# Two transformer stacks on one core: three tiles per operand slice, projections ahead of the gate, scaling on VectorE, and no barrier behind the setup

## What is computed

```python
h = rms_norm(x, norm_pre[l]);  u = h @ w_in[l]       # three attentions and their gates
y = g0 * ((oa*silu(a_z)) @ w_br_a) + g1 * ((ob*silu(b_z)) @ w_br_b) + g2 * ((oc*silu(c_z)) @ w_br_c)
x = x + rms_norm(y @ w_out[l], norm_post[l])
x = x + sigmoid(x @ w_ple_gate[l]) * (p[l] @ w_ple_proj[l])     # the "per-layer" stage
```

```python
x = x + rmsnorm(m, norm_mix_post[layer])                        # m: retention or dilated attention
f = conv_ffn(rmsnorm(x, norm_ffn_pre[layer]), ...)              # (gelu(conv(h @ w_gate)) * (h @ w_val)) @ w_down
x = x + rmsnorm(f, norm_ffn_post[layer])
if layer == 0: k_sh, v_sh = shared_kv(x, kv_norm, att_w_kv, pos)
```

## Time and profile before

| | |
|---|---|
| median of three runs | 3306.7 us (3305.99 to 3308.75) |
| the profiled execution | 3308.05 us, of it 3306.2 us in the span |
| busy: TensorE, VectorE, Pool, ScalarE | 92%, 58%, 36%, 32% of the span |
| mean granted TensorE clock | 0.972 of full |
| read from memory | 257.6 MB, 80 GB/s over the span |

### The profile page before, as it was taken

How to read it: one execution, slowest core, us unless ns; L and a number is a source line. 1 busy time by engine, 2 the same in 40 slices (tenths; PEclk the granted TensorE clock), 3 DMA queues, 4 the chain that set the end, 5 groups by cost and what they waited for, 6 DMA issues and landing times.

```text
span 3306.2 us, 38334 instructions
## 1 busy us (share of the span) xinstructions
PE 3058.2 (92%) x15088; PEld 2362.2 (71%) x15088; DVE 1909.6 (58%) x2974; ACT 1054.6 (32%) x1826; POOL 1200.1 (36%) x520
## 2 busy tenths in 40 slices
PE   5989999979899999789999989998799999979997
PEld 3766777767667777677776868886577777768885
DVE  4676554555765554555444488823666666488832
ACT  3433333234333432332222232223333333332221
POOL 2322333443222334432232444444333333244443
PEclk9999999989999999999999989999899999999998
DMA  5222222313222223232222323331222222223331
GB/s 164 64 77 64 64 77 83 90 51 99 68 74 67 71 76 90 70 98 68 64 64 64 94 70 98 96 96 51 93 77 77 77 71 77 65 69 97 96 96 64
DMA packets 78506, 262.20 MB, mean 79 GB/s; under 512 B 10910, under 2 KB 13598, under 8 KB 78200
## 3 DMA queue, kind: packets, MB, share of 16 engines
q1 hardware_dynamic: 78136, 257.60, 25.9%
q10 hardware_dynamic: 192, 2.16, 0.2%
HBM read 257.56 MB, written 6.09 MB: 80 GB/s over the span
## 4 chain that ended last, share of the span: by engine, by line
PE 80%; DVE 13%; issue 2%; ACT 2%; DMA 1%; SPq 1%; POOL 0%; ACTq 0%; DVEq 0%; POOLq 0%
PE bank L649 24%; PE bank L651 23%; PE bank L650 23%; PE bank L784 2%; PE bank L737 2%; DVE x_res L1596 1%; PE bank L764 1%; PE bank L915 1%; DVE rstd L1475 1%; PE bank L743 1%; DVE sq L1485 1%; PE bank L963 1%; PE bank L1001 0%; ACT w_hi L1094 0%; PE bank L902 0%
## 5 line engine op out<-in xcount | busy, mean ns | idle before, releaser
L509 POOL TENSOR_TENSOR w_lo<-w_raw,w_hi 128x1024 fp32r<-128x1024 f32 x462 | 1120.2, 2425 | 2046.3 <-ACT w_hi L1094 2045.9
L649 PE MATMUL bank<-h_hi,w_hi 128*128 128x512 f32 x2800 | 1152.9, 412 | 133.3 <-DVE h_lo L1586 53.4
L650 PE MATMUL bank<-h_lo,w_hi 128*128 128x512 f32 x2800 | 1107.3, 395 | 0.0
L651 PE MATMUL bank<-h_hi,w_lo 128*128 128x512 f32 x2800 | 1106.4, 395 | 0.0
L1094 ACT CAST w_hi<-w_raw 128x1024 fp32r<-128x1024 f32 x462 | 483.2, 1047 | 1328.2 <-PE bank L651 1287.7
L649 PEld LDWEIGHTS bank<-h_hi,w_hi 128*128 128x128 f32 x2800 | 534.4, 191 | 306.1 <-issue 156.7
L651 PEld LDWEIGHTS bank<-h_hi,w_lo 128*128 128x128 f32 x2800 | 534.3, 191 | 118.9
L650 PEld LDWEIGHTS bank<-h_lo,w_hi 128*128 128x128 f32 x2800 | 535.6, 191 | 106.1 <-issue 4.5
L1833 DVE TENSOR_SCALAR m<-bank,gains 128x512 f32<-128x512 f32 x48 | 36.0, 751 | 337.6 <-ACT ta L1276 200.3
L1214 ACT ACTIVATE probs<-probs,small_columns 128x128 f32<-128x128 f32 (+2 forms) x192 | 101.8, 530 | 249.8 <-DVE small_columns L1631 245.6
L649 PE MATMUL bank<-f_hi,w_hi 128*128 128x512 f32 x352 | 139.2, 396 | 0.0
(11 more groups left out here) (278 smaller groups left out, 3840.9 us busy)
## 6 DMA issues: line engine op xcount, KB each, us to landing
w_raw<-in_w SPq DMA_DIRECT2D x462, 512.0 KB, 3.6
bias_copies<-bias_vectors SPq DMA_DIRECT2D x12, 320.0 KB, 9.6
x_res<-in_x_t ACTq DMA_DIRECT2D x1, 2048.0 KB, 8.6
bias<-bias_copies SPq DMA_DIRECT2D x8, 256.0 KB, 5.7
bias<-bias_copies SPq DMA_DIRECT2D x16, 128.0 KB, 2.5
out_x<-x_res SPq DMA_DIRECT2D x8, 256.0 KB, 2.0
ple_raw<-in_p_t SPq DMA_DIRECT2D x2, 512.0 KB, 3.6
ret_decay<-in_decay SPq DMA_DIRECT2D x1, 1024.0 KB, 7.6
```

The costliest lines, as they stand in the source:

```text
L509: pool.tensor_tensor(WL[slot][:], RAW[slot][:], WH[slot][:].bitcast(F32), ALU.subtract).then_inc(sems["lo_done"], 1)
L649: pe.matmul(banks[bank][:], WH[slot][:, w], hi[:, k, :], start=start, stop=False)
L650: pe.matmul(banks[bank][:], WH[slot][:, w], lo[:, k, :], start=False, stop=False)
L651: pe.matmul(banks[bank][:], WL[slot][:, w], hi[:, k, :], start=False, stop=stop).then_inc(sems["kt_done"], 1)
```

## The change

1. `linear` behind the mixes makes three tiles together instead of two, as do the feed-forwards; in the dilated stage three of the first operand and then two of the second.
2. The per-layer stage makes the eight projections of `p` first. ScalarE moves them to a new buffer `PP`, and TensorE's banks are then freed by ScalarE's semaphores (`open_for`) and no longer by VectorE's. The operand of `p` is split in `linear`, ahead of its first tile.
3. VectorE scales the tiles of `m` itself; Pool's `scale` is gone.
4. `linear` on ScalarE ends with a square root of one column, which is not used.
5. In the feed-forward the squares are multiplied out behind the fifth tile. In the dilated stage TensorE sums the eight tiles of squares itself, ScalarE makes the second operand's upper halves between the first's, and the variance is taken after four of the second's lower halves.
6. The stage "setup" is gone: its parts stand in mix0. The table of the bias has a semaphore of its own and is loaded with the gains ahead of the weights, `X` comes in two loads, the angles and lambda are made behind the lower halves and squares of the first operand, and SyncE issues the spreading of the bias vectors as two copies, the sinks behind them, and three weight chunks behind these.

The diff, cut to its core ("..." marks what is left out; all of the removed barrier, the order of the weight stream and the renamed semaphores follow from it):

```diff
-STAGES = ["setup"]
+STAGES = []
...
-            for dst, src in ((G[:], d["gains"]), (COLS[:], d["columns"]), (ID[:], d["ident"]),
...
-                sp.dma_start(dst, src).then_inc(sems["loaded"], t.add("loaded", 16))
+            sp.dma_start(G[:], d["gains"]).then_inc(sems["gains_in"], 16)
+            for dst, src in ((OHF[:], d["oh_full"]), (OHW[:], d["oh_window"]), (TAB[0:BUCKETS, :], d["rel_bias"])):
+                sp.dma_start(dst, src).then_inc(sems["table_in"], 16)
...
+            def bias_vectors():
+                sp.wait_ge(sems["setup_step"], 3)
+                sp.dma_start(scratch[0], RVF[:]).then_inc(sems["scratch"], 16)
+                sp.dma_start(scratch[1], RVW[:]).then_inc(sems["scratch"], 16)
+                sp.wait_ge(sems["scratch"], 32)
+                for kind, first, last in ((0, 0, 4), (1, 4, BHEADS)):
+                    src = bass.AP(scratch.tensor, (kind * BHEADS + first) * RV, [[RV, last - first], [0, P], [1, RV]])
+                    fetch("spread", copies[first:last], src)
...
                 if l == 0:
-                    sp.wait_ge(sems["scratch"], 32)
-                    for h in range(BHEADS):
-                        fetch("spread", copies[h], scratch[0 if h < 4 else 1, h:h + 1, :].to_broadcast([P, RV]))
-                    load(c + RING + 1)
+                    load(c + 2 * RING)
                     sp.wait_ge(sems["spread"], t.at("spread"))
...
-            def scale(m):
...
-                for k in range(KT):
-                    pool.tensor_tensor(m[:, k, :], m[:, k, :], RSTD[:], ALU.mult).then_inc(sems["m_scaled"], 1)
...
             e.mix(l)
-            e.linear(2, KT, "post", l)
+            e.linear(3, KT, "post", l)
...
                 def ple(self, l):
-                    t.up("operand", KT)
-                    pair = [self.rotate() for _ in range(2)]
-                    self.together(pair, HH, HL, KT, KT)
                     t.up("operand", 2)
                     pe.wait_ge(sems["operand"], t.at("operand"))
-
-                    def proj():
-                        bank = self.rotate()
+                    for _ in range(KT):
+                        bank = self.open_for("p_out")
                         for k in range(2):
                             self.kt(bank, PH, PL, k, k == 0, k == 1)
-
-                    proj()
-                    proj()
-                    for _ in range(2, KT):
-                        self.whole(self.rotate())
-                        proj()
+                    t.up("operand", KT)
+                    t.up("gate", self.gates - t.k.get("gate", 0))
+                    self.together([self.open_for("gate") for _ in range(3)], HH, HL, KT, KT)
+                    for _ in range(3, KT):
+                        self.whole(self.open_for("gate"))
...
-                    pair = [self.rotate() for _ in range(2)]
-                    self.together(pair, HH, HL, KT, KT)
-                    for x in range(2, 2 * FT):
+                    self.together([self.rotate() for _ in range(3)], HH, HL, KT, KT)
+                    for x in range(3, 2 * FT):
                         self.whole(self.rotate())
-                        if x == 2:
+                        if x == 4:
                             self.all_squares(OUTB, SQ2)
...
                     self.together(opened, H2H, H2L, KT, KT)
+                    for k in range(KT):
+                        t.up("dil_squared")
+                        pe.wait_ge(sems["dil_squared"], t.at("dil_squared"))
+                        ins = pe.matmul(banks[OUTB][:], ONES[:], SQD[:, k, :], start=(k == 0), stop=(k == KT - 1))
+                    ins.then_inc(sems["summed"], t.one("summed"))
                     t.up("operand", KT)
...
+                    self.together([self.open(b) for b in DIL_FIRST_BANKS[3:5]], HH, HL, KT, KT)
...
                         act.activation((TA, TB)[tile % 2][:], banks[bank][:], ACT.Square).then_inc(sems["m_squared"], t.one("m_squared"))
+                    act.activation(sm(ROOT), ONES[:, 0:1], ACT.Sqrt).then_inc(sems["act_step"], t.one("act_step"))
+                    act.wait_ge(sems["act_step"], t.at("act_step"))
...
                 def ple(self, l):
...
+                    def proj_out(k):
+                        hi(n + 2 * k)
+                        act.wait_ge(sems["kt_done"], n + 2 * (k + 1))
+                        act.copy(PP[:, k, :], banks[(base + k) % ROTATION][:]).then_inc(sems["p_out"], t.one("p_out"))
+
+                    std()
+                    for k in range(5):
+                        proj_out(k)
                     for k in range(KT):
...
+                        act.copy(HH[:, k, :], X[:, k, :]).then_inc(sems["operand_hi"], t.one("operand_hi"))
+                        if k < 3:
+                            proj_out(5 + k)
+                        elif k == 3:
+                            hi(n + 2 * KT)
...
                     self.operands(HH, f"ffnpre{l}", True, SQ2)
+                    self.past(3, KT)
                     self.past(2, KT)
-                    self.past(1, KT)
                     std()
                     for x in range(FT):
-                        if x:
-                            self.past(2 if x > 1 else 1, KT)
+                        if x > 1:
+                            self.past(1 if x == 2 else 2, KT)
                         t.up("gate_in")
...
-                        act.activation(in_class(SQD[:, k, :]), by_class(X[:, k, :]), ACT.Square).then_inc(sems["squared"], t.one("squared"))
-                    for k in range(KT):
-                        act.activation(in_class(HH[:, k, :]), by_class(X[:, k, :]), ACT.Copy, scale=gain("kv", k)).then_inc(sems["operand_hi"], t.one("operand_hi"))
+                        act.activation(SQD[:, k, :], X[:, k, :], ACT.Square).then_inc(sems["dil_squared"], t.one("dil_squared"))
+                        for j in ((k // 2,) if k % 2 else ()) + (tuple(range(KT // 2, KT)) if k == KT - 1 else ()):
+                            act.activation(in_class(HH[:, j, :]), by_class(X[:, j, :]), ACT.Copy, scale=gain("kv", j)).then_inc(sems["kv_hi"], t.one("kv_hi"))
...
+                    def scaled(k):
+                        dve.tensor_tensor(m[:, k, :], m[:, k, :], RSTD[:], ALU.mult).then_inc(sems["dve_step"], t.one("dve_step"))
+
+                    def added(k):
+                        dve.wait_ge(sems["dve_step"], t.at("dve_step"))
+                        dve.tensor_tensor(X[:, k, :], X[:, k, :], m[:, k, :], ALU.add).then_inc(sems["x_ready"], t.one("x_ready"))
+
+                    scaled(0)
+                    added(0)
+                    for k in range(KT):
+                        if k + 1 < KT:
+                            scaled(k + 1)
+                        if target is not None:
+                            dve.wait_ge(sems["x_ready"], t.at("x_ready"))
+                            self.lo_tile(k, *target, classes=classes)
+                        if k + 1 < KT:
+                            added(k + 1)
```

260 lines of the change are left out of this document (136 added, 124 removed).

## The result

The changed kernel took 3265.1 us (median of four runs, 3263.3 to 3268.6) against 3307.3 of the kernel before beside it: a ratio of 0.9875, 95% interval 0.9863 to 0.9887. It is faster, by 42 us, where 69 were forecast; 3265 lies 11 us above the upper end of the range. The profiled execution of the changed kernel has a span of 3266.7 us, 39.5 less than before.

A forecast was written before the change was run, and what follows sets the result against it. TensorE, busy 92%, was taken as the bound, so gains come only where it stands, mostly at seams between stages. Terms 33.5 + 6 + 11 + 14.3 + 3.8 = 68.6 off 3306.7 gave 3238 us, range 3218 to 3254.

The forecast's parts named there:

- The projections hide the norm's chain: Per-layer stage, twice: 11.0 us of projection steps cover a 7.5 us chain; stage 56.1 us against 73.5, 17.4 off.
- The feed-forward seams: Start of both feed-forwards: first matmul 4.3 us earlier, 7 us gained, about 4 given back; 3 each, 6 for both.
- the two gaps: Feed-forward, ninth and tenth tile: TensorE waits near 2 us each for weight chunks cast only behind gelus.
- The end: Behind the last reciprocal: sixteen VectorE operations take 10.8 us to the last addition; 3.8 us gained (3 to 4.5).
- the squares' sum at the dilated seam: Dilated stage: TensorE's sum of squares takes 6.9 us behind 24 steps and is there at 2328.
- Setup: Start of the kernel: first scores at 58.4 us instead of 72.67, 14.3 us gained; bounds 12 and 23.
- the same sinks and copies, in two issues and in the other order: Setup's DMA queue: starts at 18, keeps the earlier 26.6 us, so the next weight chunk lands at 44.6.
- The tail of the per-layer stages: Gap behind each per-layer stage: a tanh of 0.6 us is added to the 3.5 us gap; net gain 16.7 each.
- The dilated seam: Start of the dilated stage: reciprocal near 2335.5, value-tile wait ends 11 us earlier; bounds 8 and 14.
- Untouched stages: Steady parts (attention, feed-forward loops, retention): not touched by the change and given no gain.
- Rival A: Per-layer stage: weight subtractions block VectorE, operands lag, 4 us a stage come back, dilated seam gives 8; 3249, chance 0.17.
- Rival C: Seams: saving real but lost to TensorE's lower clock at three seams and new feed-forward waits; with A 3256, chance 0.08.

## Why the prediction was right or wrong

**Right.** The projections hide the norm's chain: 57.5 us from the last sum to the end of the stage (653.8 to 711.3), against 56.1 forecast and 73.5 before. The feed-forward seams: first matmul of the stage 4.35 us sooner (a wait of 8.60 in place of 12.95; 4.3 forecast), the two gaps where they were placed (1.1 and 2.3 us), net 3.1 against 3 in the first. The end: reciprocal to last addition 10.8 us as forecast. The start of the setup's copies at 19 (18), the eight matmuls of the dilated squares 7.0 us (6.9; the profile lists two records for each, so the x8 of the earlier trace rows are four), the squares' sum at the dilated seam 40.6 us behind the last sum (39.7).

**Wrong, with the step that failed.**

1. *Setup, 14.3 forecast, 6.8 came.* The step "the same sinks and copies, in two issues and in the other order" carried 26.6 us over from the earlier trace rows. The form of the transfers decides their speed: with twelve copies the same stretch gains 13.5 us (6.6 from this edit alone), nearly the forecast. 7.5 us are missing here, of the 29 by which the spans fall short (68.6 forecast, 39.5 came).
2. *The tail of the per-layer stages, 0.7 forecast, 3.3 came, twice.* I counted the tanh and not what the change had put around it: a cast ahead of it (1.04) and a product that now has both inputs in SBUF and meets Pool (1.7). I had costed that port only in the chain and among the operands. 5.2 us, of which the cast's place gives back 1.8 to 2.7 in each stage.
3. *The dilated seam, 11 forecast, 4.6 came.* The sum of squares came as forecast. The halves behind it took 9.7 us where I allowed 4.5 or 8, and two more blocks (2.58 and 2.71 us for operations of 0.69) lay on the way to the value tile. My lower bound of 8 had no room for them. What I failed to ask is why these halves stand behind the wait at all. 6.4 us.
4. *Untouched stages, 0 forecast, -7.5 came.* The mix of layer 1 lost 2.4 us and retention 5.1 (its stretch lost 0.8 although the seam behind it gained 4.35). Of this 3.4 is the value tile above, and 2.7 in each is more matmul time at the lower clock (16.4 us against 11.0 in the mix stage, 21.8 against 16.4 in retention, halved); small waits in retention gave 1.3 back. My cause for it, the longer stand, was tested and fell. What fixes where in a stage the clock falls stays open. Over the whole kernel the clock comes to little, 1.1 us: matmuls at the lower level 80.7 us before, 82.9 after; the per-layer stages (6.3 to 3.4 each) and the dilated start (8.6 to 4.3), whose terms had the full clock in them, got back what these lost.

The first three make 19 us of the 29, the fourth 7.5, and the 1.1 us by which each per-layer stage itself fell short the rest. Rival A was nearest in mechanism (VectorE blocked by Pool), but it looked for it in the per-layer operands, where 3.5 us of slack did hold, and its 3249 has no setup term. Rival C had the clock at the seams, where it did not bind. All four errors have one sign, and I had put the range's upper end at 3254 by calling a combination of low ends rare: two of them, 2 and 3, come from one resource, the port between Pool and VectorE, so they were not independent.

On that port the Trainium skill (SBUF — State Buffer, section "SBUF: two separate sides") has the rule that the prediction applied to the chain and to the operands and not to the tail: whichever starts first holds it for its whole instruction. The 2.43 us product fits it, which began 0.46 us after Pool's subtraction and ended 0.55 us behind it.

## What to carry to other kernels

Cost a moved or merged transfer by the shape that it has after the change, and not by the bytes of the old ones. Where a wait is placed in a list of operations, ask which operations behind it don't need what it waits for, and which other engine's work they will meet once they are late. And don't price the parts of a change one by one when one makes operands early and another eats them: the same move was worth -8 us in one kernel and +14 in the other. Where a sum comes out right, check its terms by stretch: here one of 29 us did, with terms up to 3.7 us off.

## What was not expected of the hardware

- Two transfers of the same bytes as twelve, with 4 and 8 as outer dimension, left the DMA engines 0.38 busy in 27 us, with a level stretch at 0.48, and held a queue so that eight issues of half a KB took 18.8 us instead of 4.5.
- A higher granted clock on TensorE (1.00 in place of 0.87 over some 12 us) went with a later tile's being 1.8 us late: it moved Pool's work into VectorE's. Ten profiles at 1.00 show it, four at 0.87 don't.
- Beside a weight subtraction on Pool, VectorE's operations with one input in a bank kept their 0.69 us, and those with both inputs in SBUF took 2.67 in the median.
- The stands of TensorE fell by 42 us and the matmul time at the lower clock hardly moved (80.7 to 82.9 us), while between the variants it lay anywhere from 72 to 98 us; single runs of one kernel lay up to 10 us from each other.
